# Moving transposes between islands on TensorE, and splitting the last sum of a decoder layer between VectorE and GpSimd

## The chip, the core and the metric

The kernel runs on one core of a Trainium2 chip. Its time is the device time of one execution in microseconds, as the median of several runs. The time before is 584.27 us (three runs, 583.64 to 585.72).

## What is computed

One decoder layer on 512 tokens with 1024 channels, all in float32. A combined input projection feeds block-sparse causal attention (8 heads of 64) and a gated gMLP path (512 channels) side by side; both results are normalised, concatenated and projected. A squared-ReLU MLP of 4096 channels follows, and last a gated input embedding:

```python
hn = rms_norm(h, mix_pre_g[i])
proj = jnp.einsum('bsd,de->bse', hn, w_in[i])
q, k, v, u, gv = jnp.split(
    proj, [D_ATTN, 2 * D_ATTN, 3 * D_ATTN, 3 * D_ATTN + D_GMLP], axis=-1)
attn_out = moba_attention(q, k, v)
gmlp_out = gmlp_spatial_gating(jax.nn.gelu(u, approximate=False),
                               jax.nn.gelu(gv, approximate=False),
                               gmlp_ln_g[i], gmlp_ln_b[i], w_s[i], b_s[i])
mixed = jnp.concatenate([rms_norm(attn_out, attn_out_g[i]),
                         rms_norm(gmlp_out, gmlp_out_g[i])], axis=-1)
h = h + rms_norm(jnp.einsum('bse,ed->bsd', mixed, w_o[i]), mix_post_g[i])
hn = rms_norm(h, mlp_pre_g[i])
ff = jnp.square(jax.nn.relu(jnp.einsum('bsd,df->bsf', hn, w_up[i])))
h = h + rms_norm(jnp.einsum('bsf,fd->bsd', ff, w_down[i]), mlp_post_g[i])
gate = jax.nn.sigmoid(jnp.einsum('bsd,de->bse', h, w_ple_gate[i]) + b_ple_gate[i])
ple = jnp.einsum('bsp,pd->bsd', p[i], w_ple[i]) * gate
h = h + rms_norm(ple, ple_post_g[i])
```

## The kernel before

The tokens lie in four tiles of 128 (TT = 4) and the channels in eight slabs of 128 (KD = 8). The order of work is written out by hand, one program for each engine, with semaphores between them. Each engine takes its instructions strictly in that order, so whatever stands behind a waiting instruction waits too.

**Products.** Every large product is made of three matmuls per slab: both operands are split into a high and a low part of type fp32r, and `product` (L2338 on) issues high by high, low by high and high by low. ScalarE makes the high parts (`splits`, lines ending in `_hi`), VectorE subtracts to get the low ones (`_lo`), and SyncE brings raw weights. One result takes one of eight banks of PSUM. The lists in `phase_one_results` and `tail_results` give the order of the results and the bank of each; TensorE waits until the earlier user of a bank has been drained.

**Transposes.** Where a product needs its input turned, TensorE transposes four blocks of 128x128 (`turn`, L2395) into one bank, and ScalarE and VectorE write the high and the low part back to SBUF (L1415, L684). In the first phase these are the rotated queries and keys (`turn_qk`, results qkT 0 to 7) and the gated gMLP output u (`turn_gate`, gateT 0 to 3). Between them lie the products QK_T3, QK_22 and QK_T4 of a seven-product scheme for queries and keys, and the projection of v (`proj(16)` to `proj(19)`, in pieces). The queries and keys are rotated on GpSimd before their turn (`rotate`, L2084 to L2089, five short instructions for each), after VectorE's sums `qk_sum` (L804).

**Attention.** The scores of a unit, VectorE's row maxima, ScalarE's exponentials, `turn_probs` (L2558), `attend` (L2578). The inverse row sums are spread (`attn_inverse`, L897 and L899) and turned by `turn_inverse` (L2432), so that VectorE can scale the attended values.

**Gate stage and tail.** After the MLP the hidden state of each token tile is turned again (h2T 0 to 7, two for each tile), and nine gate tiles follow (`GATE_TILES`): seven of 512 columns and, for the last token tile's upper half, two of 256. The last one is called SEEDED. For each, VectorE adds the bias (L1295), ScalarE takes the sigmoid (L1972, L1969), VectorE multiplies with the embedding (`gate_ple`, L1305), ScalarE squares and sums (L1427), and VectorE multiplies by the gain (`gain_ple`, L1313). GpSimd turns the sums of squares into the reciprocal root (L2192). When it has it, `add_ple` (L1323) scales by it and adds to h, one instruction for each gate tile of the token tile, and SyncE stores each piece (L2326).

The functions that the change touches stand here in full:

## Time and profile before

| | before |
|---|---|
| median of 3 runs | 584.27 us (583.64 to 585.72) |
| the profiled execution's own time | 583.24 us |
| its span | 581.5 us |
| granted TensorE clock, mean | 0.996 |
| busy: TensorE / VectorE / ScalarE / GpSimd | 573.5 / 495.2 / 356.4 / 98.6 us |
| last product's start on TensorE | 575.12 us |

The profile is one execution of the program, in us from the span's start. A matmul's end is modelled there, so the time that one takes is read from the distance between starts. An instruction's line, as L2395, is that of the kernel before. PE is TensorE, DVE is VectorE, ACT is ScalarE, POOL is GpSimd and SP is SyncE; a q behind a name is the engine's queue.

### The profile page before, as it was taken

The numbers are of one execution on the slowest core, as the hardware profiler recorded it, in microseconds if no ns is written. First come the engines' busy times: TensorE is split into PE (matmuls) and PEld (weight loads), VectorE is DVE, ScalarE is ACT, GpSimd is POOL, SyncE is SP. The second block draws the span as 40 slices with busy tenths as digits, with TensorE's granted clock in tenths as the row PEclk, the third lists the DMA queues.
The fourth block names the chain that finished last, engine by engine and source line by source line (L and its number), as shares of the span: only waits on it lengthen the run. The fifth ranks groups of instructions, "written<-read, shape, count | busy, mean of one in ns | idle before, by whom it ended". The sixth has DMA issues, their size and how long they took to land.

```text
span 581.5 us, 8919 instructions
## 1 busy us (share of the span) xinstructions
PE 573.5 (99%) x3400; PEld 500.8 (86%) x3400; DVE 495.2 (85%) x639; ACT 356.4 (61%) x569; POOL 98.6 (17%) x152
## 2 busy tenths in 40 slices
PE   8999999999999999999999999999999999999995
PEld 7888888888888888989999999999989999988885
DVE  5899986688766998999989999999999899799664
ACT  6896675775646746667656665575655756654422
POOL 0331536000103463001010011010100100011011
PEclk9999999999999999999999999999999999999998
DMA  8982008223003559469485492774753936584011
GB/s 269 345 320 85 0 2 324 76 72 123 25 1 109 202 189 319 87 183 229 96 249 114 119 276 41 215 185 74 264 132 75 285 75 155 207 294 178 0 73 73
DMA packets 26250, 89.26 MB, mean 154 GB/s; under 512 B 3040, under 2 KB 4448, under 8 KB 25696
## 3 DMA queue, kind: packets, MB, share of 16 engines
q1 hardware_dynamic: 20448, 66.59, 32.6%
q0 software_dynamic: 4032, 14.68, 14.3%
q10 hardware_dynamic: 1728, 7.42, 3.4%
q8 instruction: 27, 0.44, 0.3%
q14 instruction: 15, 0.12, 0.1%
HBM read 82.40 MB, written 6.29 MB: 153 GB/s over the span
## 4 chain that ended last, share of the span: by engine, by line
PE 98%; DMA 1%; DVE 0%; ACT 0%; SPq 0%; issue 0%; POOL 0%; DVEq 0%; ACTq 0%
PE psum L2340 31%; PE psum L2344 30%; PE psum L2345 30%; PE psum L2395 2%; PE psum L2578 2%; PE psum L2558 2%; DMA first_raw_a<-weights_dram 1%; PE psum L2409 1%; PE psum L2432 0%; DVE h L1323 0%; ACT w_hi L1393 0%; POOL stat L2192 0%; PE psum L2463 0%; PE psum L2457 0%; PE psum L2437 0%
## 5 line engine op out<-in xcount | busy, mean ns | idle before, releaser
L2340 PE MATMUL psum<-t_hi,a_hi 128*128 128x512 f32 x216 | 84.8, 393 | 0.0
L2344 PE MATMUL psum<-t_lo,a_hi 128*128 128x512 f32 x216 | 84.6, 392 | 0.0
L2345 PE MATMUL psum<-t_hi,a_lo 128*128 128x512 f32 x216 | 84.0, 389 | 0.0
L2340 PE MATMUL psum<-w_hi,actT_hi 128*128 128x512 f32 (+1 forms) x190 | 73.6, 387 | 0.0
L2345 PE MATMUL psum<-w_hi,actT_lo 128*128 128x512 f32 (+1 forms) x190 | 72.4, 381 | 0.0
L2344 PE MATMUL psum<-w_lo,actT_hi 128*128 128x512 f32 (+1 forms) x190 | 72.3, 380 | 0.0
L2345 PE MATMUL psum<-sum_hi,up_lo 128*128 128x256 f32 x224 | 63.4, 283 | 0.0
L2344 PE MATMUL psum<-sum_lo,up_hi 128*128 128x256 f32 x224 | 63.4, 283 | 0.0
L2340 PE MATMUL psum<-sum_hi,up_hi 128*128 128x256 f32 x224 | 63.2, 282 | 0.0
L2345 PE MATMUL psum<-actT_hi,up_lo 128*128 128x256 f32 (+1 forms) x200 | 60.0, 300 | 0.0
L2344 PE MATMUL psum<-actT_lo,up_hi 128*128 128x256 f32 (+1 forms) x200 | 60.0, 300 | 0.0
L2340 PE MATMUL psum<-actT_hi,up_hi 128*128 128x256 f32 (+1 forms) x200 | 59.9, 299 | 0.0
L2142 POOL DMA_DIRECT2D raw_x<-weights_dram x21 | 18.6, 885 | 215.5 <-DVE t_lo L1130 215.1
L1189 DVE TENSOR_TENSOR acc<-acc,psum 128x512 f32<-128x512 f32 x76 | 49.0, 680 | 1.8 <-PE psum L2345 1.8
L985 DVE TENSOR_TENSOR up_lo<-raw,up_hi 128x1024 fp32r<-128x1024 f32 x37 | 46.7, 1262 | 2.6 <-ACT up_hi L1688 2.0
L2345 PEld LDWEIGHTS psum<-t_hi,a_lo 128*128 128x128 f32 x216 | 40.6, 188 | 8.9
L2340 PEld LDWEIGHTS psum<-t_hi,a_hi 128*128 128x128 f32 x216 | 40.7, 189 | 7.1
L2344 PEld LDWEIGHTS psum<-t_lo,a_hi 128*128 128x128 f32 x216 | 40.8, 189 | 6.6
L2344 PEld LDWEIGHTS psum<-sum_lo,up_hi 128*128 128x128 f32 x224 | 42.9, 191 | 1.1
L2340 PEld LDWEIGHTS psum<-sum_hi,up_hi 128*128 128x128 f32 x224 | 42.9, 191 | 1.1
L2345 PEld LDWEIGHTS psum<-sum_hi,up_lo 128*128 128x128 f32 x224 | 42.9, 191 | 0.0
L2345 PEld LDWEIGHTS psum<-w_hi,actT_lo 128*128 128x128 f32 x190 | 35.7, 188 | 6.9
(264 smaller groups left out, 1415.8 us busy)
## 6 DMA issues: line engine op xcount, KB each, us to landing
raw<-weights_dram SPq DMA_DIRECT2D x34, 512.0 KB, 4.5
raw_o<-weights_dram SPq DMA_DIRECT2D x23, 512.0 KB, 4.3
raw_x<-weights_dram POOLq DMA_DIRECT2D x21, 512.0 KB, 5.6
raw_second<-weights_dram SPq DMA_DIRECT2D x14, 512.0 KB, 4.2
raw_x<-weights_dram SPq DMA_DIRECT2D x9, 512.0 KB, 5.9
qk_raw<-weights_dram SPq DMA_DIRECT2D x8, 512.0 KB, 6.8
gate_raw<-weights_dram SPq DMA_DIRECT2D x8, 512.0 KB, 5.1
raw_o<-weights_dram POOLq DMA_DIRECT2D x7, 512.0 KB, 7.1
```

The lines of the kernel that those rows point to most:

```text
L985: nc.vector.tensor_tensor(up_lo[q % UP_SLOTS][:], block_source(step, j), up_hi[q % UP_SLOTS][:].bitcast(F32), ALU.subtract).then_inc(block ...
L1189: nc.vector.tensor_tensor(part, part, bank, how).then_inc(product_added, 1)
L2142: nc.gpsimd.dma_start(raw_x[step % 2][:], weights[down_in_stream(step, rows, half)], accum_op=ALU.add).then_inc(x_added, 16)
L2340: begin = nc.tensor.matmul(out, a_hi, b_hi, start=first, stop=False, skip_group_check=read_between)
L2344: nc.tensor.matmul(out, a_hi, b_lo, start=False, stop=False, skip_group_check=read_between)
L2345: return nc.tensor.matmul(out, a_lo, b_hi, start=False, stop=last, skip_group_check=read_between)
L2395: mm = nc.tensor.transpose(psum[:, banks[name], j * P:(j + 1) * P], source[:, j * P:(j + 1) * P], ident[:])
L2409: mm = nc.tensor.matmul(out, wsT[:, g, :], gv[:, :, g * GD:(g + 1) * GD], start=True, stop=True)
L2558: mm = nc.tensor.transpose(psum[:, bank + s, k * P:(k + 1) * P], probs[:, place_in_group(unit), s, k * P:(k + 1) * P], ident[:])
L2578: mm = nc.tensor.matmul(psum[s * DH:(s + 1) * DH, BANK_O, pair * P:(pair + 1) * P], v[:, k, head * DH:(head + 1) * DH], probsT_of[place_in ...
```

## The change

Two groups of edits, independent of each other.

First, five groups of four or eight transposes are issued elsewhere, four of them so that they join another group. gateT 0 moves behind QK_22, and gateT 1 in front of qkT 2, so that gateT 0, gateT 1 and qkT 2 stand in a row. gateT 3 moves from behind the last piece of `proj(16)` to qkT 5. The inverse of token tile 0 moves from behind `proj(18, range(2, 4))` to the probabilities of unit 0. h2T 4 and 5 move behind gate tile 1, to h2T 6 and 7. The programs of ScalarE and VectorE follow in the same order, and three banks change.

Second, the tail. The gained embedding of the last token tile's first two gate tiles (512 and 256 columns) is written to the PSUM bank of its gate tile instead of SBUF, and `add_ple` reads it from there. The last 256 columns are scaled and added by GpSimd in two instructions; the first writes to a new buffer, `last_scaled`. SyncE waits for that on a semaphore of its own.

```diff
-    first = {"proj": 0, "qkT": BANK_PT, "gateT": BANK_O}
+    first = {"proj": 0, "qkT": BANK_PT, "gateT": BANK_S + 1}
...
+    banks["gateT", 1] = banks["gateT", TT - 1] = BANK_O
...
+        def gained_of(i):
+
+            t, c0, width = GATE_TILES[i]
+            if t == TT - 1 and i != SEEDED:
+                return psum[:, bank2["gate", i], 0:width]
+            return ple_of(t)[:, c0:c0 + width]
...
+            splits(G_V * KD)
+            splits(G_V * KD + 2)
+            qk_sum(4)
+            qk_sum(5)
             dve.wait_ge(qk_lo, SPLIT_ORDER.index(QK_22) + 1)
             gate_turn_lo(0)
-            splits(G_V * KD)
-            splits(G_V * KD + 2)
+            gate_turn_lo(1)
             qkT_lo(2)
-            qk_sum(4)
-            qk_sum(5)
-            gate_turn_lo(1)
...
             splits(G_O0 * KD + 2)
+            attn_inverse(0)
             qkT_lo(6)
             qkT_lo(7)
-            attn_inverse(0)
...
-                nc.vector.tensor_tensor(ple_of(t)[:, cut], gated, gate_rows[:, 1, cut], ALU.mult
+                nc.vector.tensor_tensor(gained_of(i), gated, gate_rows[:, 1, cut], ALU.mult
...
                 for i in tiles:
+                    if i == SEEDED:
+                        continue
...
-                    nc.vector.scalar_tensor_tensor(out=h[:, t, cut], in0=ple_of(t)[:, cut],
+                    nc.vector.scalar_tensor_tensor(out=h[:, t, cut], in0=gained_of(i),
...
+            t, c0, width = GATE_TILES[SEEDED]
+            pool.wait_ge(pl_gained, SEEDED + 1)
+            after(nc.gpsimd.tensor_scalar(last_scaled[:], gained_of(SEEDED), rstd_pl[:, t:t + 1], None, ALU.mult))
+            nc.gpsimd.tensor_tensor(h[:, t, c0:c0 + width], h[:, t, c0:c0 + width], last_scaled[:], ALU.add
+                                    ).then_inc(last_ready, 1)
...
-                sp.wait_ge(out_ready, n + 1)
+                if i == SEEDED:
+                    sp.wait_ge(last_ready, 1)
+                else:
+                    sp.wait_ge(out_ready, n + 1)
...
             qk_product(QK_T3)
+            qk_product(QK_22)
             turn_gate(0)
-            qk_product(QK_22)
+            turn_gate(1)
             turn_qk(2)
-            turn_gate(1)
...
             turn_qk(5)
+            turn_gate(3)
             proj(16, range(4, KD))
-            turn_gate(3)
...
                     pe.wait_ge(*drained["mix", 3])
+                    pe.wait_ge(*drained["gateT", 2])
...
             turn_probs(0)
+            turn_inverse(0)
             proj(18, range(2, 4))
-            turn_inverse(0)
...
             gate_tile(0)
-            turn_h2(4)
-            turn_h2(5)
             gate_tile(1)
-            turn_h2(6)
-            turn_h2(7)
+            for i in range(4, 2 * TT):
+                turn_h2(i)
```

How the order on the engines changes, at the places of which the prediction speaks. The line numbers are those of each kernel.

TensorE at the end of QK_22 and the begin of QK_T4, before (`ident,u` is a group of a gateT, `ident,ln_gb` is qkT 2):

```order
L2344 MATMUL psum<-w_lo,xs_hi_96 128x512
L2345 MATMUL psum<-w_hi,xs_lo_98 128x512
L2395 MATMUL psum<-ident,ln_gb 128x128 x4
L2395 MATMUL psum<-ident,u 128x128 x4
L2340 MATMUL psum<-w_hi,actT_hi 128x512
L2344 MATMUL psum<-w_lo,actT_hi 128x512
L2345 MATMUL psum<-w_hi,actT_lo 128x512
```

The same place after:

```order
L2367 MATMUL psum<-w_lo,xs_hi_96 128x512
L2368 MATMUL psum<-w_hi,xs_lo_98 128x512
L2418 MATMUL psum<-ident,u 128x128 x8
L2418 MATMUL psum<-ident,ln_gb 128x128 x4
L2363 MATMUL psum<-w_hi,actT_hi 128x512
L2367 MATMUL psum<-w_lo,actT_hi 128x512
L2368 MATMUL psum<-w_hi,actT_lo 128x512
```

gateT 0 stands here now, 24 products later than before, with gateT 1 and qkT 2 behind it: twelve transposes in a row instead of four and eight.

VectorE from the low part of QK_T4's weights to the turn of qkT 3, before (`mixT_lo` is a gateT, `kT_lo` is qkT 2 or 3, `w_lo<-raw` are splits of the v weights, `gain_post` is `qk_sum(4)` and `(5)`):

```order
L774 TENSOR_TENSOR w_lo<-qk_raw_92,w_hi 128x2048
L804 SCALAR_TENSOR_TENSOR ln_gb<-psum,stat,ln_gb 128x512 x2
L684 TENSOR_TENSOR mixT_lo<-psum,mixT_hi 128x4x128
L666 SCALAR_TENSOR_TENSOR w_lo<-raw,cols,w_hi 128x512 x4
L684 TENSOR_TENSOR kT_lo<-psum,kT_hi 128x4x128
L804 SCALAR_TENSOR_TENSOR gain_post<-psum,stat,gain_post 128x512 x2
L684 TENSOR_TENSOR mixT_lo<-psum,mixT_hi 128x4x128
L666 SCALAR_TENSOR_TENSOR w_lo<-raw,cols,w_hi 128x512 x4
L684 TENSOR_TENSOR kT_lo<-psum,kT_hi 128x4x128
```

The same place after:

```order
L785 TENSOR_TENSOR w_lo<-qk_raw_92,w_hi 128x2048
L815 SCALAR_TENSOR_TENSOR ln_gb<-psum,stat,ln_gb 128x512 x2
L677 SCALAR_TENSOR_TENSOR w_lo<-raw,cols,w_hi 128x512 x4
L815 SCALAR_TENSOR_TENSOR gain_post<-psum,stat,gain_post 128x512 x2
L695 TENSOR_TENSOR mixT_lo<-psum,mixT_hi 128x4x128 x2
L695 TENSOR_TENSOR kT_lo<-psum,kT_hi 128x4x128
L677 SCALAR_TENSOR_TENSOR w_lo<-raw,cols,w_hi 128x512 x4
L695 TENSOR_TENSOR kT_lo<-psum,kT_hi 128x4x128
```

The four splits and the two sums moved ahead of the turns.

VectorE at the end of the program, before, from the bias of the last 512-column gate tile:

```order
L1295 TENSOR_TENSOR acc<-psum,gate_rows 128x512
L1305 TENSOR_TENSOR acc<-acc,ple_late_b 128x512
L1313 TENSOR_TENSOR ple_late_b<-acc,gate_rows 128x512
L1295 TENSOR_TENSOR acc<-psum,gate_rows 128x256
L1305 TENSOR_TENSOR acc<-acc,ple_late_b 128x256
L1313 TENSOR_TENSOR ple_late_b<-acc,gate_rows 128x256
L1305 TENSOR_TENSOR last_gated<-acc,ple_late_b 128x256
L1313 TENSOR_TENSOR ple_late_b<-last_gated,gate_rows 128x256
L1323 SCALAR_TENSOR_TENSOR h<-ple_late_b,stat,h 128x512
L1323 SCALAR_TENSOR_TENSOR h<-ple_late_b,stat,h 128x256 x2
```

The same place after:

```order
L1306 TENSOR_TENSOR acc<-psum,gate_rows 128x512
L1316 TENSOR_TENSOR acc<-acc,ple_late_b 128x512
L1324 TENSOR_TENSOR psum<-acc,gate_rows 128x512
L1306 TENSOR_TENSOR acc<-psum,gate_rows 128x256
L1316 TENSOR_TENSOR acc<-acc,ple_late_b 128x256
L1324 TENSOR_TENSOR psum<-acc,gate_rows 128x256
L1316 TENSOR_TENSOR last_gated<-acc,ple_late_b 128x256
L1324 TENSOR_TENSOR ple_late_b<-last_gated,gate_rows 128x256
L1336 SCALAR_TENSOR_TENSOR h<-psum,stat,h 128x512
L1336 SCALAR_TENSOR_TENSOR h<-psum,stat,h 128x256
```

Two gains write to PSUM, the sums read from there, and the third sum is gone.

GpSimd at the end of the program, after; before, it ends with the second root to `stat`:

```order
L2205 TENSOR_TENSOR stat<-stat 128x1
L2192 TENSOR_SCALAR stat<-stat 128x1 x2
L2196 TENSOR_TENSOR last_gated<-stat 128x1
L2205 TENSOR_TENSOR stat<-stat 128x1
L2212 TENSOR_SCALAR last_scaled<-ple_late_b,stat 128x256
L2213 TENSOR_TENSOR h<-h,last_scaled 128x256
```

The last two rows are new and wait for VectorE's last gain.

## Rows read from the trace of the kernel before

**Rows 1.** The page, busy us, share of the span, count.

```profile
PE 573.5 (99%) x3400; PEld 500.8 (86%) x3400; DVE 495.2 (85%) x639; ACT 356.4 (61%) x569; POOL 98.6 (17%) x152
```

**Rows 2.** Busy time by stretch: us, then each engine's busy us (count), clock, DMA.

```profile
81.00:120.00 39.00, 39.00 (x245) 32.80 (x244) 28.54 (x40) 24.31 (x56) 13.25 (x30) 1.00 0.41 149
...
504.00:581.50 77.50, 71.39 (x354) 60.21 (x352) 56.93 (x83) 33.41 (x66) 9.08 (x21) 0.97 0.35 129
```

**Rows 3.** TensorE in time: start, us of all, engine, line, operation (group of four).

```profile
79.80 0.39 PE L2340 MATMUL psum<-w_hi,xs_hi 128*128 128x512 f32 x1
...
81.16 0.60 PE L2395 MATMUL psum<-ident,u 128*128 128x128 f32 x4
...
82.31 0.39 PE L2340 MATMUL psum<-w_hi,xs_hi 128*128 128x512 f32 x1
```

**Rows 4.** TensorE in time, a group of eight.

```profile
87.08 0.60 PE L2395 MATMUL psum<-ident,ln_gb 128*128 128x128 f32 x4
87.52 0.60 PE L2395 MATMUL psum<-ident,u 128*128 128x128 f32 x4
...
88.65 0.39 PE L2340 MATMUL psum<-w_hi,actT_hi 128*128 128x512 f32 x1
```

**Rows 5.** In time, about the inverse of token tile 0.

```profile
109.17 0.40 ACT L1614 ACTIVATE probs<-psum,stat 128x128 f32<-128x128 f32 x1
...
111.31 0.47 PE L2340 MATMUL psum<-w_hi,actT_hi 128*128 128x512 f32 x1
...
111.62 0.43 DVE L899 COPY act_hi_free<-rinv 128x512 f32<-128x512 f32 x1
```

**Rows 6.** The chain that ended last: start, us, what.

```profile
577.48 0.75 DVE h L1323
...
578.62 0.39 DVE h L1323
```

**Rows 7.** The stores' line from 578 us on.

```profile
L2326 SPq DMA_DIRECT2D out_dram<-h x3: 332/412/452, 578.3 to 579.1; - x3
```

**Rows 8.** In time, VectorE and GpSimd about the rotations.

```profile
84.22 0.68 DVE L684 TENSOR_TENSOR mixT_lo<-psum,mixT_hi 128x512 fp32r<-128x512 f32 x1
...
84.82 3.06 DVE L666 SCALAR_TENSOR_TENSOR w_lo<-raw,cols,w_hi 128x512 fp32r<-128x512 f32 x4
...
88.95 1.40 DVE L804 SCALAR_TENSOR_TENSOR gain_post<-psum,stat,gain_post 128x512 f32<-128x512 f32 x2
...
84.90 0.83 POOL L2087 TENSOR_TENSOR ln_gb<-rope_tmp 128x64 f32<-128x64 f32 x1
85.70 0.76 POOL L2089 TENSOR_TENSOR ln_gb<-rope_tmp 128x64 f32<-128x64 f32 x1
...
89.84 0.46 POOL L2084 TENSOR_TENSOR rope_tmp<-gain_post,rope_sb 128x128 f32<-128x128 f32 x1 [0.81 <-DVE gain_post L804]
```

**Rows 9.** GpSimd's groups by line: count, ns, names.

```profile
L2125 POOL TENSOR_TENSOR actT_lo<-xr,actT_hi x4: 1273/1292/1747, 183.0 to 190.8; 128x512 fp32r<-128x512 f32 x4
...
L2071 POOL TENSOR_SCALAR_AFFINE_SELECT wsT<-wsT 128x1024 f32<-128x1024 f32 x1 | 1.1, 1101 | 0.1
```

**Rows 10.** The program's closing instructions, line 274: count, ns min/median/max, starts.

```profile
L274 DVEq DRAIN  x1: 1576/1576/1576, 577.5 to 577.5; - x1
L274 POOLq DRAIN  x1: 2352/2352/2352, 577.6 to 577.6; - x1
...
L274 SPq DRAIN  x1: 7/7/7, 581.3 to 581.3; - x1
```

**Rows 11.** In time, the gate stage's first tiles.

```profile
536.63 1.15 ACT L1391 ACTIVATE w_hi<-gate_raw 128x512 fp32r<-128x512 f32 x2
542.00 1.09 ACT L1415 ACTIVATE actT_hi<-psum 128x512 fp32r<-128x512 f32 x2 [4.21 <-PE psum L2395]
...
538.12 1.28 DVE L663 TENSOR_TENSOR w_lo<-gate_raw,w_hi 128x512 fp32r<-128x512 f32 x2
...
541.36 1.04 PE L2395 MATMUL psum<-ident,h 128*128 128x128 f32 x8
```

16 lines of the change are left out of this document (9 added, 7 removed).

## The prediction, made before the changed kernel ran

> **What bounds the kernel now.** I read the page's busy shares first, then TensorE in order of time around its transposes, then the chain that ended last, and last the queues that close the program. TensorE is busy for 573.5 of 581.5 us [rows 1]. In the first stage that the change touches, 81 to 120 us, it is busy for 39.00 of 39.00; in the second, from 504 to the end, for 71.39 of 77.50, and the 6.11 left are the tail behind its last product [rows 2]. So time can leave in two ways only: TensorE issues in less time, or the tail, from 575.4 to 581.5, gets shorter. What VectorE, ScalarE and GpSimd gain elsewhere is hidden. The profiled execution took 583.24 us with a span of 581.5; that is 1.03 us under the median of the runs, 584.27, and I carry the same distance over.
>
> **The transposes.** Six products of 512 columns run from 79.80 to 81.16, so one takes 0.227 and a step of three 0.68 [rows 3]. A lone group of four transposes starts at 81.16, and the fourth product behind it at 82.31: 1.15 us, less three products (0.68), leaves 0.47 for the group and both changes of kind [rows 3]. A double group starts at 87.08 with its fourth product at 88.65: 1.57 less 0.68 is 0.89 [rows 4]. Four transposes inside a run take 0.44, from 87.08 to 87.52 [rows 4]. So the transposes themselves cost what they cost anywhere, and what a merge removes is 2 x 0.47 - 0.89 = 0.05, or 0.47 - 0.44 = 0.03 by the other subtraction. No transpose is removed: the words "four groups fewer" are about groups, and the work stays.
> - gateT 0 moves behind the product QK_22 to gateT 1 and qkT 2: 0.03 to 0.05.
> - gateT 3 moves from in front of the scores to qkT 4 and 5: the same, if the step from the projection's tile shape to that of the scores costs behind a product what it costs behind a transpose. No row of this kernel has it behind a product, so 0 and 0.1 are its ends.
> - h2T 4 to 7 form one group of sixteen: 0.03 to 0.05.
> - The inverse of tile 0 moves to the probabilities of unit 0, but the attention products that stood behind it remain an island of their own between the same two projections. So I count 0, with 0.05 as the other end.
>
> Together 0.09 to 0.20; I take 0.12, because three merges are real and the 0.03 comes from the subtraction with the smaller rounding. The outer ends are 0 and 0.25.
>
> **The waits that the moves add.** Each moved group has to find its inputs ready and its bank free.
> - QK_22 starts 0.47 earlier, at 81.16, and gateT 0 and 1 stand ahead of qkT 2. qkT 2 would then start at 87.08 - 0.47 + 2 x 0.44 = 87.49. It waits for GpSimd's rotation, which ends at 86.46 now [rows 8]. But VectorE no longer has the turn at 84.22 ahead of its four splits (84.82, 3.06 us) [rows 8], so these start about 0.6 earlier. Beside them GpSimd's instructions on 64 columns take 0.83 and 0.76, while one on 128 columns takes 0.46 beside VectorE's sum out of PSUM at 88.95 [rows 8]. Two or three more of the five instructions of a rotation then lie beside splits, at 0.3 more each: 87.1 to 87.4, just ahead of the 87.49. I count no wait, with 0.3 us as the other end.
> - Behind qkT 2 in TensorE's queue stands QK_T4; both its inputs and VectorE's later work have far longer slack, and the sums for qkT 4 and 5 now come earlier.
> - The inverse is wanted at 111.31, where the next product started [rows 5]. VectorE had it at 111.62 + 0.43 = 112.05, behind two turns. The swap in VectorE's order lets it start when the last exponentials end, at 109.57 [rows 5]; even with the 0.66 of reciprocal and copy that is 110.3, so 1 us of cover. Without the swap in VectorE's order it would have cost 0.7.
> - h2T 4 and 5 come 5.5 us later, at 541.36 - 0.89 = 540.47 [rows 11]. In the queues of ScalarE and VectorE the last two slabs of the gate weights stand behind their turns. The fifth's transposes end at 541.35, ScalarE takes 1.09 for two turns and 1.15 for two slabs, VectorE 1.28 for two slabs [rows 11]: the fifth turn is done by 542.0, the slabs on ScalarE by 543.2, and on VectorE both by 544.0 to 544.6 instead of 539.4. Gate tile 2 reaches them six steps after 542.2, at 546.3. Cover of 1.7 us or more; no cost.
>
> **The tail.** When GpSimd has the last root, VectorE adds 512 columns from 577.48 (0.75) and twice 256, the last from 578.62 for 0.39, to 579.01 [rows 6]. At first sight the change takes 0.39 away. It does not, because of SyncE: it issues three stores, from 578.3 on, that take 0.33, 0.41 and 0.45 us to issue [rows 7]. The second goes out at 578.65, as soon as its columns are added, and holds the queue until 579.06; the third starts at 579.11 [rows 7]. The third is already bound by the issue of the second, so VectorE's 0.39 lies beside it and the gain is at most 0.05. Sources in PSUM change little: VectorE's sums of 512 columns out of PSUM take 1.40 for two that overlap [rows 8], 0.70 each against the 0.75 of one alone here. I count 0.01.
>
> What GpSimd adds must end before 579.07. It starts at about 577.55, 0.07 behind VectorE because it waits for its own semaphore (an estimate: two instructions of its own without a wait overlap, 84.90 + 0.83 against 85.70 [rows 8]), scales, waits 0.1 on itself, adds. A two-input instruction on 512 columns takes 1.29 [rows 9] and one on 128 takes 0.46 [rows 8], so 0.74 for 256. For the scaling with one input no such row stands. The lower bound is 0.28, a quarter of 1.10, the select on 1024 columns [rows 9]; the upper one is 0.74, as if it had two inputs. I take 0.45, nearest to the select with a fixed part. That ends at 577.55 + 0.45 + 0.1 + 0.74 = 578.84, 0.23 ahead of SyncE. With 0.74 for the scaling it is 579.13, some 0.06 late.
>
> The Trainium skill, GPSIMD Engine Reference, Performance versus the Vector engine, speaks against such a move: it gives elementwise work to VectorE, with GpSimd about twice as slow. The trace agrees and is harsher: my 1.19 for the two instructions against the 0.39 of VectorE. By that rule alone the sum would rise; it does not only because the queue hides it.
>
> One thing comes after it. GpSimd's closing drain takes 2.35 us from 577.6, to 579.98, with none of its own work under way, while VectorE's (1.58 from 577.5) ends with its last sum at 579.07 [rows 10]. If those 2.35 are a fixed cost, the end of GpSimd moves with its last instruction, from 577.45 to 578.84, by 1.39 to 581.37, just past SyncE's drain at 581.29 [rows 10]. That costs 0.05 to 0.1; I take +0.06.
>
> **Sum.** -0.12 (transposes) - 0.01 (sums) + 0.06 (drain) = -0.07. So 583.17 for the profiled execution and 584.2 for the median.
>
> **The rivals.**
> - *GpSimd is shut out by VectorE, slower.* Where VectorE reads two operands of SBUF, GpSimd's short instructions double [rows 8]. If the sums out of PSUM blocked it too, it would start only at 578.6 and end at 579.95; the last store would be 0.85 late and the drain would end near 582.5, so +1.1 and about 585.3. It decides from 0.25 us of blocking on. Against it speaks the 0.46 beside the sum at 88.95 [rows 8]. The Trainium skill, SBUF — State Buffer, Who interferes with whom, states that a VectorE instruction with at most one SBUF input outside its two-port modes does not contend with GpSimd; by it this rival is out. 6 in 100. Even this stays within 0.3% (1.75 us), about what a measurement of this kernel can tell from no change.
> - *A moved group waits, slower.* If qkT 2 waits for the rotation and one more turn finds its copy late, 0.3 to 0.6: 584.5 to 584.8. To be slower by over 1.75 the gate stage would have to lose its 1.7 us of cover and as much again: about 586.2. 12 in 100 for the small one, 3 for the large.
> - *The queue is not the bound, faster.* If the second store is issued in 0.33 as the first, the third starts when its columns are there, and 0.1 more is gained; with 0.25 from the transposes: 583.9. 15 in 100.
> - *The switch is dearer than the rows tell* (a drained array whose cost shows elsewhere), over 0.4 a group: 582.4. The steady 0.68 before and behind a group speaks against it. 4 in 100.
> - *The forecast:* no difference that can be measured, 60 in 100.
>
> **How the numbers follow.** Forecast, small wait, small gain and blocked GpSimd, 93 in 100 together, all lie within 0.3%. Faster by over 0.3% 0.04, slower 0.03. The range takes in the bounds (-0.3, +1.1) and the spread of the runs before (583.64 to 585.72) in part: 583.2 to 585.4.
>
> **What would show it.** In the profile after: TensorE's last product ends near 575.3 instead of 575.4, with a group of twelve transposes near 86.6 and one of sixteen near 540.5; a fourth product behind a group comes at 0.68 plus 0.109 per transpose plus 0.02 to 0.03. In the tail SyncE's last issue is at 579.0, GpSimd's two instructions add to 1.0 to 1.5, and its drain ends last. Wrong would be: a span changed by over 0.5 us, a gap of TensorE ahead of qkT 2 or in gate tile 2, a scaling that takes over 1 us, or a last store that moves with GpSimd.

## The result, and the profile after

| | before | after |
|---|---|---|
| median of 22 executions each, us | 583.51 | 584.16 |
| fastest, us | 583.00 | 583.62 |
| profiled execution, span, us | 581.5 | 582.0 |

The ratio of after to before is 1.0013, with a 95% interval of 1.0007 to 1.0019. The change makes the kernel slower; the medians differ by 0.65 us. That is within the 0.3% that was called no difference, but on the other side of the forecast of -0.07 us, and with this many executions it can be told from nothing. A ratio in this document is estimated from the single executions; it isn't the quotient of the two medians beside it, and differs from that by up to 0.0006.

That 584.16 stands beside the forecast 584.2 is luck. The forecast was built on a median of three executions, 584.27, and over 22 executions the median of the same kernel is 583.51. So only times taken side by side are compared. The profiled execution of before is the one of the rows shown above.

The first line answers to [rows 1]: busy time, share of the span and count by engine. VectorE has one instruction fewer (638 for 639), GpSimd two more. The two lines under it answer to [rows 2]; in the second stretch TensorE's busy time goes from 71.39 to 71.26, since its last product comes 0.13 us earlier. Whether that is a gain of the change is asked below.

```profile
PE 574.0 (99%) x3400; PEld 501.7 (86%) x3400; DVE 495.2 (85%) x638; ACT 356.4 (61%) x569; POOL 99.2 (17%) x154
```

```profile
81.00:120.00 39.00, 39.00 (x245) 32.71 (x244) 28.56 (x40) 24.39 (x56) 12.87 (x30) 1.00 0.39 149
504.00:581.50 77.50, 71.26 (x354) 60.18 (x352) 56.46 (x82) 33.34 (x66) 10.76 (x23) 0.99 0.36 129
```

TensorE in order of time in after: start, us, line. They answer to [rows 3] and [rows 4]: the lone group at 81.16 is gone, twelve transposes stand together at 86.51, and the gate stage has one run of sixteen.

```profile
86.51 1.04 PE L2418 MATMUL psum<-ident,u 128*128 128x128 f32 x8
87.39 0.60 PE L2418 MATMUL psum<-ident,ln_gb 128*128 128x128 f32 x4
87.74 0.48 PE L2363 MATMUL psum<-w_hi,actT_hi 128*128 128x512 f32 x1
...
88.53 0.39 PE L2363 MATMUL psum<-w_hi,actT_hi 128*128 128x512 f32 x1
...
540.39 1.91 PE L2418 MATMUL psum<-ident,h 128*128 128x128 f32 x16
...
542.83 0.39 PE L2363 MATMUL psum<-w_hi,actT_hi 128*128 128x512 f32 x1
```

The change isn't the only thing that moves these starts. The product that starts at 79.80 in [rows 3] lies ahead of every moved group. The same product in after, and in the regroupings alone (the first experiment below):

```profile
79.70 0.39 PE L2363 MATMUL psum<-w_hi,xs_hi 128*128 128x512 f32 x1
```

```profile
79.54 0.39 PE L2341 MATMUL psum<-w_hi,xs_hi 128*128 128x512 f32 x1
```

By the trace's nanoseconds after is 0.091 us ahead there and the regroupings alone 0.255, and nothing has been changed up to that point. It is scatter of the start: the three other profiled kernels with before's order of work (the tail alone, the spare GpSimd work, before with a copy) are 0.06 to 0.29 ahead at the same product.

The tail of after in order of time answers to [rows 6] and [rows 7]. VectorE's two sums start together with GpSimd's scaling, and the first of the three stores is issued at 578.12:

```profile
576.76 0.55 POOL L2205 TENSOR_TENSOR stat<-stat 128x1 f32<-128x1 f32 x1 [1.04 <-ACT junk_late L1440]
577.35 1.14 DVE L1336 SCALAR_TENSOR_TENSOR h<-psum,stat,h 128x512 f32<-128x512 f32 x2 [0.74 <-POOL stat L2205]
577.41 0.95 POOL L2212 TENSOR_SCALAR last_scaled<-ple_late_b,stat 128x256 f32<-128x256 f32 x1
578.12 1.41 SPq L2349 DMA_DIRECT2D out_dram<-h  x3
578.45 0.72 POOL L2213 TENSOR_TENSOR h<-h,last_scaled 128x256 f32<-128x256 f32 x1
```

The closing instructions and the stores' own line (count, ns min/median/max, starts) answer to [rows 10] and [rows 7]; the last line is the time from a store's issue to its landing, us min/median/max.

```profile
L275 POOLq DRAIN  x1: 3142/3142/3142, 578.4 to 578.4; - x1
L275 SPq COMPARE_BRANCH  x1: 38/38/38, 581.6 to 581.6; - x1
L275 SPq DRAIN  x1: 7/7/7, 581.8 to 581.8; - x1
```

```profile
L2349 SPq DMA_DIRECT2D out_dram<-h x3: 332/332/416, 578.1 to 579.2; - x3
DMA to landing us min/median/max: 2.0/2.3/2.4
```

The difference of the two spans adds up like this, measured from the start of TensorE's last product (575.115 before, 574.984 after, by the trace's nanoseconds). The last product starts 0.131 earlier, but 0.091 of that is the scatter of the start, so 0.04 is left for the regroupings. GpSimd's add ends at 579.175, and the third store is issued 4.218 behind the last product where it was 3.991: +0.227. SyncE sees it landed 2.417 behind the issue where it was 2.025: +0.392. The sum is +0.488, the difference of the spans. GpSimd's closing drain ends at 581.552, 0.23 ahead of SyncE's own drain, and decides nothing here.

So two things need a cause: a scaling of 0.953 us where 0.45 was forecast, and a landing that takes 0.4 longer. A third is where the forecast 0.12 of the regroupings went.

### The profile page after: what moved, and what is told of

Its sections match the earlier page's. It is cut to its first block, busy times and chain, and to the rows that moved or that the text cites. A ratio compares the mean times of both kernels' runs of the same rounds, so it can differ in the third digit from the quotient of the medians.

```text
span 582.0 us, 8921 instructions
## 1 busy us (share of the span) xinstructions
PE 574.0 (99%) x3400; PEld 501.7 (86%) x3400; DVE 495.2 (85%) x638; ACT 356.4 (61%) x569; POOL 99.2 (17%) x154
## 4 chain that ended last, share of the span: by engine, by line
PE 98%; POOL 0%; issue 0%; DVE 0%; ACT 0%; POOLq 0%
PE psum L2363 31%; PE psum L2367 30%; PE psum L2368 30%; PE psum L2418 2%; PE psum L2602 2%; PE psum L2582 2%; PE psum L2472 1%; PE psum L2432 1%; PE psum L2455 0%; POOL last_scaled L2212 0%; POOLq L275 0%; PE psum L2480 0%; PE psum L2483 0%; POOL last_gated L2196 0%; POOL stat L2205 0%
```

## Experiments: the two halves apart

**Regroupings alone.** The edit is the diff without its tail (no `last_scaled`, no wait of SyncE on GpSimd).

> The moved transposes of the change without its tail, which is the tail of before. Theory 1 (the moves are worth what TensorE's starts show, and the whole loss is in the tail): 0.13 us faster than before, 0.02 to 0.03 at each of four places and the rest in the noise of the first products; the last product starts near 574.98 instead of 575.12, span 581.3 to 581.4. Rival (the moves cost something that the one trace of the change does not show, by which its median of 22 runs lies 0.65 above before though its profile lies 0.50 above): 0.1 to 0.3 slower.

583.78 (11 executions) against 583.47, ratio 1.0007 [0.9998, 1.0016]. The tail is before's, landing 2.017. TensorE's last product comes 0.27 earlier in the profiled execution, but 0.255 of that is there ahead of the first moved group; the regroupings give 0.01. The 0.13 us of theory 1 isn't there, and the interval doesn't tell between no gain and a small loss.

**Tail alone.** The rest of the diff.

> The new tail of the change with the order of before. Theory 1: slower than before by what the change lost plus what the moves gave, 0.65 + 0.13 = 0.8 us: the last store is issued near 579.33 instead of 579.11 and lands 2.4 after its issue instead of 2.0, so the span is near 582.1. Rival (the loss belongs to the moves): within 0.1 of before.

584.37 (11) against the same 583.47, ratio 1.0017 [1.0008, 1.0026]: the tail alone has the whole loss. Scaling 0.951, add 0.722, third issue at 579.250, landing 2.400.

## Experiments: what GpSimd's two instructions cost

**Spare GpSimd work in before's tail.** The same scaling and an add of two operands into scratch; nobody waits for them, and VectorE keeps its three sums.

```diff
+            after(nc.gpsimd.tensor_scalar(last_scaled[:], ple_of(t)[:, c0:c0 + width], rstd_pl[:, t:t + 1], None,
+                                          ALU.mult))
+            after(nc.gpsimd.tensor_tensor(last_summed[:], last_scaled[:], last_scaled[:], ALU.add))
```

> The kernel before with two spare instructions on GpSimd behind the last root (scale 256 columns, add 256 columns, into scratch that nobody reads); VectorE and SyncE do all that they did. Theory 2 (what lengthens the landing and the end is that GpSimd ends later and fetches its closing instructions while the last store moves): the last store is still issued at 579.11, lands 2.3 to 2.5 after its issue, a fetch on the instruction queue lies at 579.5 to 579.9, and the time is 0.3 to 0.5 above before. Theory 3 (the end is late only because SyncE waits for GpSimd): the landing stays at 2.0 and the time within 0.1 of before, unless GpSimd's drain itself ends last. Beside VectorE's sums out of SBUF the scaling should also take as long or longer than the 0.95 of the change, if sharing with VectorE is what lengthens it.

584.42 (11) against 583.47, ratio 1.0020 [1.0011, 1.0029]. The row of its scaling, and its closing rows:

```profile
L2202 POOL TENSOR_SCALAR last_scaled<-ple_late_b,stat 128x256 f32<-128x256 f32 x1 | 1.5, 1502 | 0.1
```

```profile
L274 POOLq COMPARE_BRANCH  x1: 33/33/33, 579.7 to 579.7; - x1
L274 POOLq DRAIN  x1: 2352/2352/2352, 579.8 to 579.8; - x1
L274 SPq COMPARE_BRANCH  x1: 38/38/38, 581.2 to 581.2; - x1
```

The last store landed 1.996 behind its issue, so theory 2 fell; the fetch came at 577.870. The stores had landed by 581.2, but the program ended at 582.4, behind GpSimd's drain of the same 2352 ns as in [rows 10]. The close is a fixed cost behind GpSimd's last instruction, as the prediction took it. Here 2.2 us of work that nobody reads made the end 1.0 us later (7.400 behind the last product, in before 6.398). Beside VectorE's sums with both tensor operands in SBUF the scaling took 1.502, and VectorE's second sum 0.702 instead of 0.476.

**The price alone.** After, with spare GpSimd instructions at quiet places; two theories, that the scaling costs 0.95 by itself, or that VectorE's sums hold it up.

> The changed kernel with four spare instructions on GpSimd in the gate stage, each where VectorE either idles or reads at most one operand of SBUF: a scaling by a column of 256 columns (near 564.6), one of 128 columns (near 572.8), a scaling by a constant of 256 columns and a sum of two operands of 256 columns (from 569.5). Theory A (the scaling by a column takes its 0.95 us by itself): 0.95 for 256 columns, 0.55 to 0.6 for 128; the scaling by a constant tells whether the column is what costs. Theory B (VectorE's first sum out of PSUM shut it out until 578.10, and it then took 0.27): 0.3 to 0.45 for 256 columns. The sum of two operands takes 0.72 in both. No effect on the time.

One execution, 583.9 us. GpSimd in order of time: a scaling by a column (256 columns), one by a constant, a sum of two operands, and at the end a scaling by a column of 128 columns:

```profile
564.56 0.96 POOL L2198 TENSOR_SCALAR probe_out<-gate_rows,stat 128x256 f32<-128x256 f32 x1
...
569.97 0.89 POOL L2218 TENSOR_SCALAR probe_out<-gate_rows 128x256 f32<-128x256 f32 x1 [1.93 <-DVE h L1338]
570.94 0.61 POOL L2219 TENSOR_TENSOR probe_out<-gate_rows 128x256 f32<-128x256 f32 x1
...
573.35 0.62 POOL L2200 TENSOR_SCALAR probe_out<-gate_rows,stat 128x128 f32<-128x128 f32 x1
```

The scaling takes 0.96 in a stretch where VectorE is idle for 0.70 us of it: the price is its own, and VectorE's sums out of PSUM cost it nothing (0.953 beside them). The Trainium skill, SBUF — State Buffer, Who interferes with whom, says that a VectorE instruction with one SBUF input at most, outside its two-port modes, leaves GpSimd alone and that one with two contends with a GpSimd instruction that reads SBUF; 0.953 here and 1.502 in the kernel with the spare work agree. What the bounds had missed is the order: on GpSimd one input and a column (0.96) is dearer than two inputs (0.61).

**Scaling on ScalarE**, GpSimd only adds:

```diff
+            act.wait_ge(pl_rstd, t + 1)
+            act.wait_ge(pl_gained, SEEDED + 1)
+            nc.scalar.activation(last_scaled[:], gained_of(SEEDED), ACT.Copy, scale=rstd_pl[:, t:t + 1]
+                                 ).then_inc(root_ready, 1)
...
-            pool.wait_ge(pl_gained, SEEDED + 1)
-            after(nc.gpsimd.tensor_scalar(last_scaled[:], gained_of(SEEDED), rstd_pl[:, t:t + 1], None, ALU.mult))
+            pool.wait_ge(root_ready, 2)
```

> The changed kernel with the scaling of the last 256 columns on ScalarE, which is idle there, and only the addition on GpSimd. If the scaling on GpSimd (0.95 us where 0.45 was forecast) and the late end of GpSimd are what the change lost: ScalarE scales from 577.37 for 0.42, GpSimd adds from 577.85 to 578.57, the third store is issued at 578.93 as the queue comes free, GpSimd's drain ends at 580.95 and no longer last; the span is 581.1 to 581.4 and the time 0.6 to 0.9 below that of the change, so 0.0 to 0.3 below before. Rival (any work of GpSimd there costs, because its fetch of instructions then meets the stores): the landing of the last store stays at 2.4 and the span at 581.5 or more.

584.28 (11) against 583.47, ratio 1.0012 [1.0003, 1.0021]. SyncE's third issue came 0.461 behind its second, as before's does (0.456): the queue is the bound again, and still nothing is gained, for the landing took 2.822.

**Scaling as a product** of two tensors, the column repeated along the row:

```diff
-            after(nc.gpsimd.tensor_scalar(last_scaled[:], gained_of(SEEDED), rstd_pl[:, t:t + 1], None, ALU.mult))
+            after(nc.gpsimd.tensor_tensor(last_scaled[:], gained_of(SEEDED),
+                                          rstd_pl[:, t:t + 1].to_broadcast([P, width]), ALU.mult))
```

> The changed kernel with GpSimd's scaling written as a product of two tensors, the root's column repeated along the row. If the form of the instruction costs (0.95 for a scaling by a column and 0.89 by a constant, but 0.61 to 0.72 for two operands of 256 columns): 0.6 to 0.75 us instead of 0.95, the third store issued near 578.95 instead of 579.20, GpSimd's drain ends 0.2 to 0.3 earlier, and the span is 0.15 to 0.3 shorter than that of the change. If the form does not matter: 0.95 again and the time of the change.

584.16 (10), ratio 1.0013 [1.0004, 1.0023]. The scaling took 0.612, GpSimd was done ahead of SyncE, the third issue came 0.462 behind the second, and the landing took 2.665. With the price mended, all of the tail's loss is in the landing.

## Experiments: why the last store lands later

The landing is 2.0 us in some of these kernels and 2.4 to 2.8 in the others. Where it is late, one packet of another queue lies among the stores' packets: q14, which fetches instructions, 8 KB. DMA of the last microseconds in GB/s, in 40 slices, before first and then after; the last line of each is the packets, MB and share of that queue.

```profile
GB/s 0 0 0 0 0 0 0 0 0 66 0 0 0 0 0 0 115 344 426 410 377 410 328 385 377 394 377 246 8 0 0 0 0 0 0 0 0 0 0 0
...
q14 instruction: 1, 0.01, 0.4%
```

```profile
GB/s 0 0 0 0 0 0 0 0 0 0 0 0 0 0 0 115 393 377 442 360 418 377 369 262 164 344 377 164 25 25 8 8 25 8 0 0 0 0 0 0
...
q14 instruction: 1, 0.01, 0.8%
```

Both stretches are 577 to 582, a slice is 0.125 us. In before the fetch is the lone slice of 66 GB/s at 578.17, ahead of the stores. In after it starts at 579.673 among them, and the stores end in a tail of 25 and 8 GB/s. That these are the packets of the one DMA engine that served the fetch is my inference; no row names the engine.

**GpSimd waits on its own add**, so that its stream ends later; the theory was that the fetch follows GpSimd's last instruction.

> The changed kernel with one more instruction on GpSimd, a wait for its own last addition; nothing else moves. If what lengthens the landing of the last store from 2.0 to 2.4 us is a fetch of GpSimd's instructions at 579.7, in the middle of that store: with the wait the fetch goes out earlier, near 577.8, as in the kernel with spare work, and the landing is 2.0 again, while the end is still set by GpSimd's drain, 2.5 behind its addition, so the span stays within 0.1 of the change's 582.0. If the landing is late because SyncE issues the store late or alone: 2.4 again.

One execution, 584.08 us: the fetch stayed among the stores (580.018), landing 2.440. The theory fell.

**No GpSimd work in the tail, one store fewer**: the regroupings, and the last two pieces of 256 columns summed and stored as one of 512.

```diff
                 for i in tiles:
+                    if i == SEEDED - 1:
+                        continue
                     cut = slice(GATE_TILES[i][1], GATE_TILES[i][1] + GATE_TILES[i][2])
+                    if i == SEEDED:
+                        cut = slice(GATE_TILES[SEEDED - 1][1], D)
...
+                if i == SEEDED - 1:
+                    continue
+                if i == SEEDED:
+                    n, c0, width = n - 1, GATE_TILES[SEEDED - 1][1], W
```

> The moved transposes with the tail of before, but the last two gate tiles' 256 columns each are scaled, added and stored as one piece of 512 by VectorE and SyncE. If the third store was bound by SyncE's issue of the second (0.41 us) and GpSimd's end sets nothing here: VectorE ends at 578.75 instead of 579.02, the one store is issued there and lands 2.0 to 2.1 later, the last landing is 0.2 to 0.3 earlier, the span 581.0, and the time 0.3 to 0.5 below before. Rival (the last store's size decides): it lands 2.2 or more after its issue and nothing is gained.

584.77 (11), ratio 1.0018 [1.0009, 1.0027]. The last issue did come earlier, 3.805 behind the last product instead of 3.991, but this is the worst landing of all, 3.191, with the fetch at 581.553 and before's tail on GpSimd. So GpSimd isn't the cause. What this kernel shares with after, and with no kernel that lands in 2.0, is VectorE's count of 638.

**Half the columns.** As after, but VectorE takes 128 of the 256 columns in a third sum, GpSimd the other 128. VectorE's count is 639 again.

> As after, but of the last 256 columns GpSimd takes only the last 128; VectorE scales and adds the 128 ahead of them, after its other two sums. GpSimd's pair should then cost about what was forecast for 256 columns: .62 us for the scaling (measured for 128 columns) and, by 2.6 ns for a column less, some .4 us for the sum, so that it ends near 578.55 us, and VectorE ends near 578.85. SyncE's third issue is then held by its second again: .45 us after 578.52, at 578.97 to 579.0, .11 to .14 us earlier than before. Theory A (the price of the scaling alone made it slower; the store lands 2.0 us after its issue): end of the last store near 581.0 to 581.1, the median 583.35 to 583.45. Theory B (the landing grows to 2.4 us as soon as GpSimd works into the time of the stores, since the fetch of instructions that follows its last instruction falls among them): the end is near 581.4, 583.7 to 583.8, ratio 1.0003 to 1.0006. GpSimd's own close, 2.35 us after its last instruction, ends at 581.0 and decides in neither.

583.69 (11) against 583.41, ratio 1.0002 [0.9993, 1.0011]. GpSimd worked until 579.150, into the time of the stores (from 578.69), though not as long as in after: 3.60 behind the last product, where it was 4.19. The fetch came at 578.392 and the landing took 1.974, so my theory B in that expectation (any work of GpSimd there makes the landing late) fell. The third issue was at 579.596, 4.041 behind the last product, so not earlier than in before either.

**One instruction more on VectorE.** The direct test: after, and nothing but a copy of one column behind the sums.

```diff
+                if t == TT - 1:
+                    nc.vector.tensor_copy(last_gated[:, 0:1], rstd_pl[:, t:t + 1])
```

> After, with one instruction more on VectorE behind its last two sums: a copy of one column between two tiles in SBUF, which nobody waits for. The traces so far part in two: where VectorE's stream has 639 timed instructions (before, the moves alone, the spare GpSimd work, the half tail) the last fetch of instructions (queue q14, 8 KB) starts .4 to .8 us after VectorE's first sum starts and the last store lands 2.0 us after its issue; where it has 638 (after, the tail alone, both other ways to scale, the one wide store) the fetch starts 1.6 us or more after the last sum and the store lands 2.4 to 3.2 us after its issue. Theory F (the place in VectorE's program at which that fetch is made moved with the one instruction fewer): the fetch is back near 578 us, the third store issued near 579.20 lands after 2.0 us, at 581.2, GpSimd's close at 581.55 then ends last, and the median falls by .2 to .3 us against after's, to 583.9 or 583.95, ratio 1.0006 to 1.0010. Rival R (the fetch follows GpSimd's or the stores' time): fetch at 579.7, landing 2.4, ratio 1.0012 to 1.0014.

583.83 (12) against 583.45, ratio 1.0004 [0.9996, 1.0013]. The fetch started at 579.682, 0.50 behind the first sum, ahead of the stores (580.0), and the last store landed 1.895 behind its issue. GpSimd's add ended 4.19 behind the last product, as in after, so its work didn't move the fetch. GpSimd's close now ends last (at 583.392; SyncE's drain is at 583.1):

```profile
L275 POOLq DRAIN  x1: 3142/3142/3142, 580.2 to 580.2; - x1
L275 SPq COMPARE_BRANCH  x1: 38/38/38, 582.9 to 582.9; - x1
```

```profile
L2351 SPq DMA_DIRECT2D out_dram<-h x3: 332/332/417, 580.0 to 581.0; - x3
DMA to landing us min/median/max: 1.9/2.0/2.1
```

(All starts are 1.8 later here: this execution was the slowest of the twelve, with waits of TensorE near 81 and 260 us. From the last product to the end it took 6.799, after 7.016. The times alone can't tell it from after: the two intervals overlap.)

**The same copy with one wide store.**

> The four regroupings and the tail of before with the last two pieces of 256 columns summed and stored as one of 512, as in the earlier experiment whose store landed 3.19 us after its issue, and again one instruction more on VectorE that nobody waits for. Theory F (the fetch among the stores, which came with VectorE's one instruction fewer, held the landing up): landing 2.0 to 2.1 us, the end 1.1 us earlier than in that experiment, ratio .9997 to 1.0004 where it was 1.0018. Rival R (a store of 256 KB that is issued late lands in 3 us by itself): ratio 1.0015 to 1.002 again.

583.18 (12) against 583.45, ratio 0.9996 [0.9987, 1.0004]. One instruction more, and the ratio goes from 1.0018 to 0.9996 (584.77 and 583.18), with intervals that don't overlap. First the stores without the copy, then with it:

```profile
L2335 SPq DMA_DIRECT2D out_dram<-h x2: 332/332/332, 579.1 to 579.7; - x2
DMA to landing us min/median/max: 2.0/2.6/3.2
```

```profile
L2337 SPq DMA_DIRECT2D out_dram<-h x2: 332/332/332, 579.8 to 580.4; - x2
DMA to landing us min/median/max: 2.0/2.0/2.0
```

How a fetch of one packet holds a store up for so long isn't shown. In after, the stores' last packet starts 0.54 later behind the issue than in before, more than the 0.39 that the landing grew. Without the copy here the fetch comes at the very end of the stores: one packet of four bytes is left to start behind it, 0.49 later than with the copy, and the landing follows that packet by 1.05 us where it follows by 0.36 with the copy. So late packets explain 0.49 of the 1.17 us between these two landings, and 0.68 stays open.

**The tail of after, both failures mended**: the product form, the copy, and the three regroupings other than the first.

> The three regroupings other than the first; the tail of after with the scaling done as a product with the column repeated along the row (.61 us measured for it instead of .95); one instruction more on VectorE. Theory F: GpSimd ends near 578.85, SyncE's third issue is held by its second and comes near 579.0, the landing takes 2.0 us, GpSimd's close ends at 581.2: the end some .1 us earlier than before's, which with .06 to .09 us of the regroupings gives a median of 583.25 to 583.4, ratio .9996 to .9998. Rival R (late landing, as when the product was tried first): ratio 1.0006 to 1.0010.

583.43 (12) against 583.45, ratio 0.9996 [0.9987, 1.0005]. Landing 2.0, and the third issue 3.992 behind the last product where before's is 3.991: SyncE's second issue holds it, as the prediction had it. The third sum's 0.39 us was never there to be won.

**The copy in before.**

> Before, with the same one instruction more on VectorE behind its last sum and nothing else. Theory F in its plain form (the fetch is made when VectorE's stream reaches a certain place ahead of the last sums; what stands behind does not move it): fetch and landing as in before, ratio .9998 to 1.0002. Theory F2 (only the count of 639 gives the early fetch; 640 would be as bad as 638): landing 2.4, ratio 1.0006 to 1.0010. In both the copy itself is hidden, since SyncE's third issue is held by its second.

583.52 (12) against 583.45, ratio 0.9999 [0.9991, 1.0008], landing 2.026 with VectorE's count at 640. What stands behind the sums doesn't spoil the early fetch; one instruction too few does.

Over the one profiled execution of each of the twenty kernels there is no exception: with 639 or 640 instructions the last landing takes 1.9 to 2.0 (thirteen kernels), with 638 it takes 2.4 to 3.2 (seven: after, the tail alone, the kernel with the spare instructions for the price, both other ways to scale, the own wait, the one store without the copy). That the fetch is VectorE's own I infer from this; no row names the engine. It fits that GpSimd's wait on itself and ScalarE's scaling, each an instruction more on another engine, left the fetch late, and that four more instructions on GpSimd moved the fetch before the last one (575.4 to 570.6) and not the last (579.7 in both). Why one instruction fewer moves it from 0.5 us behind the first sum to behind the last one isn't shown.

## Experiments: what the first regrouping costs

**All but the first regrouping**, **the first alone**, and **all again**; before's tail in each.

> The tail is that of before and, of the four regroupings, the first is left out: the transposes of the gate's first two token tiles stand apart again, with the second up-projection-sized product (QK_22) between them, as before; the other three regroupings stay. It asks why the moves alone brought nothing in the times (1.0007) though the trace of one execution had TensorE's last product .13 to .27 us earlier. Theory A (the moved product QK_22 now stands first and has sometimes to wait for its operand, since the .45 us of transposes that stood ahead of it are gone; seen once as a wait of .50 us): without that regrouping no execution can have this wait, the three merges that are left give .06 to .09 us, and the median is 583.3 to 583.5, ratio .9997 or below. Theory B (all regroupings are worth what the trace shows, and the median of the moves was only scatter): ratio .9998 to 1.0000, the same as the first regrouping alone. Theory C (one of the other three costs something in most executions): ratio above 1.0005.

> The tail and three of the regroupings are as before; only the first regrouping is made: QK_22 ahead of the transposes of the gate's first two token tiles, which follow each other. Theory A (QK_22 loses its cover and waits for its operand in some executions, by up to .5 us): ratio 1.0003 to 1.001 with a wider scatter than before. Theory B (only scatter): .02 to .03 us faster, ratio 1.0000. In the profiled execution the gap ahead of QK_22's first product (near 80.6 us) is what tells: under .05 us where the operand was there, some tenths where not.

> The same kernel as the first experiment: all four regroupings, the tail of before. More executions of it, beside those with the first regrouping left out and with it alone. Theory A (the first regrouping costs in some executions): between 1.0002 and 1.001, and slower than the kernel with the first regrouping left out by .0005 or more. Theory B (scatter): ratio .9998, as the .13 us of the trace have it, within .0005 of the other two.

Against 583.41: without the first 583.59, ratio 0.9997 [0.9988, 1.0006]; the first alone 583.74, 1.0001 [0.9992, 1.0010]; all four 583.83, 1.0004 [0.9995, 1.0013]. The order is the one of theory A, but the intervals overlap.

The traces say more, for every one of the four. Each kernel issues 3400 products and transposes on TensorE, and outside of the moved groups the same number is the same product. The table has how much a profiled execution loses (+) or gains (-) over a stretch against the execution of before, us by the starts of the same product at both ends (times of before):

| stretch | regrouping in it | executions that have it | those that don't |
|---|---|---|---|
| 79.9 to 92 | the first | -0.02 (eight), -0.01 (one), +0.53 to +0.71 (four) | 0.00 to +0.29 |
| 92 to 108 | gateT 3 | +0.01 to +0.06, mean +0.03 | -0.03 to +0.01, mean -0.01 |
| 108 to 118 | the inverse | +0.01 to +0.02 | 0.00 |
| 535 to 550 | h2T 4 to 7 | -0.05 to -0.01, mean -0.02 | 0.00 |

So the first and the last gain about 0.02 each, the two in the middle lose 0.03 and 0.01, and together they bring nothing even where nothing goes wrong. Why gateT 3 costs where a merge gains elsewhere wasn't tried.

The four executions with +0.53 to +0.71 are another matter. The first rows are VectorE in the kernel with the first regrouping alone, the second TensorE there:

```profile
77.52 1.68 DVE L844 TENSOR_SCALAR u<-u,stat 128x512 f32<-128x512 f32 x4 [1.20 <-POOL stat L2043]
80.31 1.22 DVE L760 TENSOR_TENSOR xs_lo<-xT_raw,xs_hi 128x1024 fp32r<-128x1024 f32 x1
```

```profile
81.09 0.39 PE L2346 MATMUL psum<-w_hi,xs_lo 128*128 128x512 f32 x1
81.63 0.47 PE L2341 MATMUL psum<-w_hi,xs_hi 128*128 128x512 f32 x1 [0.16 <-issue]
```

In some executions VectorE waits 1.20 us for GpSimd from 76 us on, and the low half of QK_22's operand (`xs_lo`) comes at 81.5 instead of 80.0. With QK_22 moved ahead of gateT 0, TensorE then steps 0.54 instead of 0.23 at 81.09. In before's order the group of transposes covers it; in the execution of before with the copy, VectorE was as late:

```profile
77.08 1.68 DVE L843 TENSOR_SCALAR u<-u,stat 128x512 f32<-128x512 f32 x4 [1.20 <-POOL stat L2044]
```

```profile
80.64 0.39 PE L2347 MATMUL psum<-w_hi,xs_lo 128*128 128x512 f32 x1
80.87 0.60 PE L2397 MATMUL psum<-ident,u 128*128 128x128 f32 x4
81.22 0.48 PE L2342 MATMUL psum<-w_hi,xs_hi 128*128 128x512 f32 x1
```

VectorE was late in this way in seven of the twenty profiled executions, with either order. In the four with QK_22 moved, TensorE waited 0.32, 0.32, 0.32 and 0.50 us for it. In two of the three without it did not wait at QK_22; in the third (the product form with the copy) the transposes' cover was just too short, and it waited 0.14. With the group at 87, where some more is lost, and the slower steps behind a wait, the four lose 0.53 to 0.71 us by 92 us, the three 0.11, 0.12 and 0.29. So the lost cover costs some 0.4 us in such an execution, and 0.14 on the mean if seven in twenty are of this kind (an estimate).

**One wide store without and with the first regrouping**, both with the copy.

> The three regroupings other than the first, the last two pieces summed and stored as one of 512 columns, and one instruction more on VectorE; against the next kernel it lacks only the first regrouping. If the first regrouping costs its cover in some executions (waits of .2 to .5 us ahead of QK_22, seen in 3 or 4 of 12 traces), this one is .05 to .3 us faster than the next on the mean and .1 to .4 us faster than before: ratio .9992 to .9996. If that regrouping costs nothing, the two are equal, both near .9996. As the fetch falls ahead of the stores, the landing of the last store is 2.0 to 2.1 us.

> The kernel with all four regroupings, one store of 512 columns and one instruction more on VectorE again, beside the one without the first regrouping. Ratio .9996 as before if its median holds (583.2), a landing of 2.0 to 2.1 us; the same as the other kernel of this call if the first regrouping costs nothing, up to .3 us behind it on the mean if it does.

583.17 and 583.31 (12 each) against 583.41, both 0.9996 [0.9985, 1.0006]; landing 2.019 in both. The one without is 0.14 ahead, in the direction of theory A and too little to be told from nothing. These are the fastest kernels found: with one store fewer, the last issue comes 3.805 behind the last product instead of 3.991.

## Why the prediction was wrong, step by step

- *Transposes, -0.12.* Wrong, though the last product starts 0.131 earlier. That this matches the forecast is luck: 0.091 of it is there ahead of the first moved group. The price of a change of kind was right. From 86.51 to 88.53 is 2.02; less three products (0.68) and twelve transposes at 0.109 leaves 0.03, as said, and the first and the h2T regrouping gain 0.02 each. What failed is the count of three such merges: gateT 3, for which no row stood and a gain was taken all the same, loses 0.03, and the inverse, put at 0, loses 0.01. The sum of the four is 0.00.
- *Waits of the moved groups, 0.* Wrong in one place, and not the one that was priced. I asked whether qkT 2 would find its rotation; the step "QK_22 starts 0.47 earlier" was never followed to QK_22's own operand. VectorE is 1.2 us late in seven of the twenty profiled executions, and the lost cover costs some 0.4 there, so 0.14 on the mean. The wait and the lost cover are shown by the traces; the times are in their direction but don't prove the size.
- *VectorE's 0.39 is hidden by SyncE.* Right, and shown three times over (third issue 0.461, 0.462 and 0.459 behind the second once GpSimd is in time).
- *Sums out of PSUM, -0.01; the add, 0.74; the start 0.07 behind VectorE.* Right, or nearly: the sums take 0.751 and 0.474 (in before 0.750 and 0.477, so nothing is gained), the add 0.723, and the starts are 577.415 and 577.346.
- *The scaling, 0.45, ends 0.28 and 0.74.* This term was mis-sized: 0.953. The upper end stood on the idea that one input can't cost more than two; the row of a select gave the lower one. With 0.95 in my own sum GpSimd ends at 579.34 and the third store is 0.27 late; measured from the last product it was 0.227. The step that failed is taking rows of other operations as bounds.
- *GpSimd's close, +0.06.* The mechanism was right, 2.35 fixed (2352 ns again with spare work), but it doesn't decide in after, where SyncE's drain comes 0.23 later behind the late landing; it does decide once the landing is mended (by 0.3 us in after with the copy).
- *The landing, not in the sum.* I carried over 2.0 us for the last store without saying so. It became 2.417, because VectorE's one instruction fewer put an instruction fetch among the stores. No row of before spoke against the 2.0, and it is 0.39 of the 0.62 that the tail lost: the largest term of the miss is one that the sum didn't have.
- *The rivals.* GpSimd wasn't shut out (0.953 beside VectorE, 0.957 alone). The one on the other side that came true, a late last store, was in my list of what would be wrong, "a scaling that takes over 1 us, or a last store that moves with GpSimd", but had no price or chance of its own.

Together: -0.13 at the last product (0.09 of it the scatter of the start), +0.23 and +0.39 in the tail make the +0.49 of the profiled executions. For the times the scatter falls out. The regroupings give 0.00 to -0.04, the tail +0.62, and the wait at QK_22, which the profiled execution of after doesn't have, adds some 0.14 on the mean: +0.72 to +0.76, where the medians differ by 0.65 and the ratio says 0.4 to 1.1.

## What to carry to other kernels

Before work is handed to GpSimd at the end of a program, measure that very operation at that width, and count its fixed close behind the last instruction, even if nobody waits for the result. When a step is moved ahead of another, ask for the moved step's own inputs in a bad execution, not only for those of what it is moved to. Before an earlier last product is booked as a gain, take off what was there ahead of the first edit. And when the last transfer lands later without being larger, look for an instruction fetch among its packets: adding one idle instruction is a cheap test. Here it took 0.2 and 1.2 us off the end of the profiled executions, and 0.3 and 1.6 off the medians.

## What the runs showed that I had not expected

- On GpSimd, 256 columns of float32: by a column 0.957, by a constant 0.887, as a product with a repeated column 0.612, a sum of two tensors 0.612 to 0.723. By a column with 128 columns 0.617, so 2.7 ns a column over a fixed 0.28.
- A single 8 KB instruction fetch among the last stores goes with a landing of 2.4 to 3.2 us instead of 2.0. The Trainium skill, DMA: Bandwidth & Descriptors, Queues, rings and completion order, says that a DMA engine takes turns between its queues by whole packets; the tail of 25 and 8 GB/s in after may be such a turn, and no run here shows that it is.
- TensorE waits near 259 us for VectorE's sums of the accumulator, by 0.3 to 0.5 us, in nine of the twenty profiled executions, with either order of the work (that of before with the copy among them). In those nine ScalarE's split of one slab of weights (`t_hi` from `raw_o`) began at 230.6 to 232.1, in the eleven others at 229.8 to 230.9. What delays it wasn't tried; it is a part of the scatter of 1 us that every kernel here has.
